# The last-ranked expert of a mixture moved to the third turn, with unsplit weights, in the two column halves of TensorE

## The reference, cut to what matters

```python
logits = (xt @ router).astype(jnp.float32)
top_logit, top_idx = lax.top_k(logits, TOP_K)          # 2 of 8 experts for each of 256 tokens
gates = jax.nn.softmax(top_logit, axis=-1)
...
out[token] += gate * ((silu(x @ w1[e]) * (x @ w3[e])) @ w2[e])   # w1, w3: 1024 x 1408, w2: 1408 x 1024
```

## Time and profile before

| what | before |
|---|---|
| median of 3 runs | 1899.74 us (1897.98 to 1900.82) |
| profiled execution | 1896.1 us, its span 1894.1 us |
| mean granted clock of TensorE | 0.988 |
| PE busy | 1841.9 us (97%) |
| DVE, ACT, POOL busy | 1331.0, 917.2, 63.0 us |
| HBM to SBUF, mean | 170 GB/s |

### The profile page before, as it was taken

The page is one execution under the profiler, slowest core; times in us unless marked ns, Lnnn a source line. Parts: engine busy times, 40 slices in busy tenths (PEclk is TensorE's granted clock), DMA queues, the critical chain, the costliest instruction groups (busy, mean ns, idle before and its releaser), DMA issues.

```text
span 1894.1 us, 35005 instructions
## 1 busy us (share of the span) xinstructions
PE 1841.9 (97%) x14961; PEld 1729.7 (91%) x14961; DVE 1331.0 (70%) x1900; ACT 917.2 (48%) x1072; POOL 63.0 (3%) x32
## 2 busy tenths in 40 slices
PE   9899999999998999999999999999999999989999
PEld 9889999999997999999999888888889988889988
DVE  7975566755589656667564768888879678666675
ACT  5353345433453433434434566777766544444453
POOL 0000000000000000000101010111110000000000
PEclk9899999999998999999999999999999999999999
DMA  8221246455542214535545578899965423324330
GB/s 316 91 90 57 90 167 222 162 193 180 181 159 90 74 57 139 193 138 189 194 154 187 200 238 291 323 332 329 337 249 180 154 90 102 124 99 159 122 122 24
DMA packets 52826, 321.89 MB, mean 170 GB/s; under 512 B 6336, under 2 KB 9664, under 8 KB 20032
## 3 DMA queue, kind: packets, MB, share of 16 engines
q1 hardware_dynamic: 52240, 317.76, 47.8%
q10 hardware_dynamic: 432, 1.90, 0.3%
HBM read 317.01 MB, written 1.05 MB: 168 GB/s over the span
## 4 chain that ended last, share of the span: by engine, by line
PE 80%; DVE 13%; ACT 4%; issue 3%; DMA 0%; POOL 0%; DVEq 0%; ACTq 0%; SPq 0%; POOLq 0%
PE b L393 78%; DVE s_arena L409 5%; DVE s_ring_lo L516 3%; ACT s_wh L418 2%; PE b L2553 1%; DVE s_arena L1442 1%; PE b L2089 0%; DVE s_arena L652 0%; DVE s_arena L412 0%; DVE s_arena L2588 0%; DVE s_roots L409 0%; ACT s_arena L418 0%; DMA s_ring<-experts 0%; POOL s_ring_lo L516 0%; DVE s_Hl L409 0%
## 5 line engine op out<-in xcount | busy, mean ns | idle before, releaser
L516 DVE TENSOR_TENSOR s_ring_lo<-s_ring,s_wh 128x2048 fp32r<-128x2048 f32 (+3 forms) x316 | 661.6, 2098 | 302.3 <-ACT s_wh L418 300.9
L418 ACT ACTIVATE s_wh<-s_ring 128x2048 fp32r<-128x2048 f32 (+3 forms) x332 | 574.1, 1732 | 273.7 <-PE b L393 265.9
L393 PE MATMUL b<-s_Hh,s_wh 128*128 128x256 f32 x2184 | 636.2, 291 | 3.8 <-DVE s_arena L409 1.2
L393 PE MATMUL b<-s_Hl,s_wh 128*128 128x256 f32 x2184 | 618.8, 283 | 0.0
L393 PE MATMUL b<-s_Hh,s_ring_lo 128*128 128x256 f32 x2184 | 618.6, 283 | 0.0
L393 PEld LDWEIGHTS b<-s_Hh,s_wh 128*128 128x128 f32 x2184 | 419.4, 192 | 13.6 <-issue 4.7
L393 PEld LDWEIGHTS b<-s_Hl,s_wh 128*128 128x128 f32 x2184 | 419.8, 192 | 1.1
L393 PEld LDWEIGHTS b<-s_Hh,s_ring_lo 128*128 128x128 f32 x2184 | 419.3, 192 | 0.0
L393 PE MATMUL b<-s_arena_r,s_wh 128*128 128x256 f32 x1536 | 277.0, 282 | 6.7 <-DVE s_arena L409 1.7
L393 PEld LDWEIGHTS b<-s_arena_r,s_wh 128*128 128x128 f32 x1536 | 235.5, 188 | 9.4 <-DVE s_arena L409 2.1
L393 PE MATMUL b<-s_arena_r,s_ring_lo 128*128 128x256 f32 x768 | 215.4, 280 | 0.0
(11 more groups left out here) (198 smaller groups left out, 1776.1 us busy)
## 6 DMA issues: line engine op xcount, KB each, us to landing
s_ring<-fixed SPq DMA_DIRECT2D x158, 1024.0 KB, 4.9
s_ring<-experts SPq DMA_DIRECT2D x95, 1024.0 KB, 5.3
s_ring<-experts SPq DMA_DIRECT2D x48, 768.0 KB, 4.6
s_ring<-fixed SPq DMA_DIRECT2D x24, 256.0 KB, 4.2
s_c<-c SPq DMA_DIRECT2D x1, 1664.0 KB, 17.6
s_ring<-fixed SPq DMA_DIRECT2D x3, 512.0 KB, 6.1
s_arena<-s_arena SPq DMA_DIRECT2D x48, 32.0 KB, 3.1
s_c<-c ACTq DMA_DIRECT2D x1, 1344.0 KB, 5.6
```

Source lines behind the costliest of these rows:

```text
L393: return e.matmul(out, l, r, start=start, stop=True, skip_group_check=True)
L418: return e.activation(out, x, ACT.Copy, scale=scale)
L516: e.tensor_tensor(l_, r_, h_.bitcast(F), SUB).then_inc(*up(engine, z % "lo", i))
```

## The change

Turn 2 is now the last-ranked expert, and ranks 2 to 6 follow as turns 3 to 7 (`RANK`). So the turn with two sets, whose second is packed, is turn 3. The new turn 2 (`NARROW`) has one set of at most 64 rows. Its tokens stay in full fp32 (`n_H`, `n_hid`), its 18 weight pieces are neither rounded nor split (`unsplit`), and each block of 128 rows of the contraction is one full-precision matmul with 64 stationary columns. Even blocks write partitions 0 to 63 of the bank, odd ones 64 to 127, and the two halves are added where the packed set adds its high and low sums (`packed_dve`, through `gate_low`, `up_low`) or, for w2, by the scatter, whose placing matrix holds the 64 places twice. The groups of the gathers become (2), (3), (4, 5), (6, 7).

```diff
-SETS = (2, 2, 2, 1, 1, 1, 1, 1)
+RANK = (0, 1, 7, 2, 3, 4, 5, 6)
+SETS = (2, 2, 1, 2, 1, 1, 1, 1)
 DENSE = 2
-GROUPS = ((2,), (3, 4), (5, 6), (7,))
+NARROW = 2
+GROUPS = ((2,), (3,), (4, 5), (6, 7))
...
             for j in range(0 if i == 0 else i + AHEAD, min(i + AHEAD + 1, len(LOADS))):
-                if j not in late_pieces:
+                if j not in late_pieces and j not in unsplit_pieces:
                     round_piece(e, j)
...
-        PACKED = {(2, 1)}
+        PACKED = {(3, 1)}
+        HALF = PACKED | {(NARROW, 0)}
...
         GATHERS = {1: [(0, 0), (0, 1), (0, 2), (0, 3)], 2: [(1, 0), (1, 1), (1, 2), (1, 3)],
-                   3: [(2, 0), (2, 1)], 4: [(2, 2), (2, 3)], 5: [(3, 0), (3, 1)], 6: [(3, 2), (3, 3)]}
+                   3: [(2, 0), (2, 1), (2, 2), (2, 3)], 4: [(3, 0), (3, 1)], 5: [(3, 2), (3, 3)]}
...
-                    out[9 + s if p > DENSE else 10 + s].append(("turn", p, 0, s))
-                    out[14 + s].append(("turn", p, 1, s))
+                    out[9 + s if p > DENSE else 11].append(("turn", p, 0, s))
+                    out[15 if p == NARROW else 14 + s].append(("turn", p, 1, s))
...
+        def unsplit(e, i):
+
+            e.wait_ge(landed[i % RAW], 16 * (i // RAW + 1))
+            return raw_of(i).rearrange("p (k n) -> p k n", k=LOADS[i].kt)
...
                 for kk in range(4):
+                    if p == NARROW:
+                        last = mm(e, b[HALVES[kk % 2], 0:width], n_H[:, 4 * h + kk, :], wv[:, kk, :], h == 0 and kk < 2)
+                        continue
...
                 for k in range(4 * j, min(4 * j + 4, 11)):
+                    if p == NARROW:
+                        last = mm(e, b[HALVES[k % 2], :], n_hid[:, k, :], wv[:, k - 4 * j, :], k < 2)
+                        continue
...
-                for half in range(2):
+                for half in range(2 if p != NARROW else 0):
                     rest_piece(e, li["xd", (p, half, 2)], "G")
```

More of the change, by code:

```diff
@@ L503, in build @@
         even_late = [li["eg", 0], li["eg", 1]] + [li["eo.2", j] for j in range(6)]
-        pool_pieces = {li["xd", (p, half, 2)] for p in range(8) for half in range(2)}
+        pool_pieces = {li["xd", (p, half, 2)] for p in range(8) for half in range(2) if p != NARROW}
+        unsplit_pieces = {j for j, piece in enumerate(LOADS) if piece.turn == NARROW}
         def rest_piece(e, i, engine):
@@ L526, in rests @@
             for j in range(0 if i == 0 else i + AHEAD, min(i + AHEAD + 1, len(LOADS))):
-                if j not in pool_pieces and j not in late_pieces:
+                if j not in pool_pieces and j not in late_pieces and j not in unsplit_pieces:
                     rest_piece(e, j, "V")
@@ L1824, in build @@
         GROUP_OF = {p: g for g, ps in enumerate(GROUPS) for p in ps}
-        PLACES = [sum(64 if (p, s) in PACKED else 128 for p in ps for s in range(SETS[p])) for ps in GROUPS]
+        half_units = [t for t, (p, ch, s) in enumerate(UNITS) if (p, s) in HALF]
+        PLACES = [sum(64 if (p, s) in HALF else 128 for p in ps for s in range(SETS[p])) for ps in GROUPS]
         GATHERS = {1: [(0, 0), (0, 1), (0, 2), (0, 3)], 2: [(1, 0), (1, 1), (1, 2), (1, 3)],
-                   3: [(2, 0), (2, 1)], 4: [(2, 2), (2, 3)], 5: [(3, 0), (3, 1)], 6: [(3, 2), (3, 3)]}
-        PLACED = {1: 0, 2: 1, 3: 2, 5: 3}
+                   3: [(2, 0), (2, 1), (2, 2), (2, 3)], 4: [(3, 0), (3, 1)], 5: [(3, 2), (3, 3)]}
+        PLACED = {1: 0, 2: 1, 3: 2, 4: 3}
         STEPS = 24
@@ L1871, in job_end @@
         def job_end(job):
+            if job[0] == "turn" and job[1] == NARROW or job[0] == "gather" and job[1] == GROUP_OF[NARROW]:
+                return {"turn": "hid hi", "gather": "slot hi"}[job[0]], *job[1:]
             return {"turn": "hid lo", "scatter": "spread", "gather": "slot lo", "place": "PT", "tokens": "token lo", "wide": "gates wide"}[job[0]], *job[1:]
@@ L2043, in place_pe @@
             for blk in range(2):
-                last = mm(e, b[:, 256:257], m_P[g % 2][:, blk, o:o + 128].bitcast(F), m_gp[:, blk, p:p + 1], blk == 0)
+                last = mm(e, b[:, 256:257], m_P[g % 2][:, blk, o:o + 128].bitcast(F), m_gp[:, blk, RANK[p]:RANK[p] + 1], blk == 0)
             last.then_inc(*up("PE", "P turned", p, s))
@@ L2150, in expert_down_pe @@
             i = li["xd", (p, half, j)]
-            wv = wts(i)
-            e.wait_ge(*on("lo", i))
+            if p == NARROW:
+                wv = unsplit(e, i)
+            else:
+                wv = wts(i)
+                e.wait_ge(*on("lo", i))
             for s in range(SETS[p]):
@@ L2424, in moe_dve @@
                     for job in jobs[i]:
+                        if job_end(job)[0] in ("hid hi", "slot hi"):
+                            continue
                         if job[0] == "tokens":
@@ L3347, in sync_program @@
                     e.wait_ge(*on("experts known"))
-                    who[piece.turn] = e.value_load(m_int[0:1, piece.turn:piece.turn + 1], min_val=0, max_val=7)
+                    who[piece.turn] = e.value_load(m_int[0:1, RANK[piece.turn]:RANK[piece.turn] + 1], min_val=0, max_val=7)
                 if i == 2:
```

42 lines of the change are left out of this document (25 added, 17 removed).

## The result

| what | before | after |
|---|---|---|
| median of the runs taken together | 1899.07 us (1894.9 to 1901.11, 6 runs) | 1885.34 us (1881.24 to 1890.11, 6 runs) |
| ratio | | 0.9932, 95% interval 0.9918 to 0.9945 |
| profiled execution | 1896.1 us, span 1894.1 | 1881.24 us, span 1879.3 |
| first to last 512-column matmul of the mixture | 1044.50 to 1393.17, 348.7 us | 1041.86 to 1378.41, 336.5 us |

What follows compares the result with a forecast made beforehand. PE was taken to bound the kernel: 16.4 us saved in products, less 2.4 for changes of shape and 1.5 for waits, gives -12.5 us. The forecast median was 1887.2 us, range 1882.5 to 1892.

Steps and rivals of the forecast that it cites:

- What bounds: Whole kernel: PE is the bound, busy 97% of the span; transfers are the next limit.
- The slot: Turn 2's products: an even and an odd block run side by side, 0.86 us at 512 columns, 29.3 us in all.
- Rival 3: Turn 2's products: the column halves take turns, products 56.8 us, time 1913, slower; chance 0.07.
- Changes of shape: PE switching to 64 columns and back: 0.14 us in, 0.09 out; with 64-partition runs and turned chunks, cost 2.4.
- Rival 2: Turn 2's slots: weight loads do not overlap and cost 9.7 us, leaving gain 2.8, time 1897; chance 0.03.
- The waits: PE in turns 2 and 3: narrow pieces cover less of other engines' work, together +1.5 us of waiting.
- the wait at `place`: Step 15 of turn 2: PE waits 1.1 us at the first `place` for ACT's and DVE's chain ending in the gather.
- the add: Second scatter of turn 2: PE waits 0.6 us for the add of the first scatter.
- the first split piece: Turn 3's first piece, rounded after the gather's copies: of the order of 0.3 us may show, inside the 1.1's error.
- Transfers: Turn 2 to turn 3's first piece: 7 MB land in 26 us against PE's 28, covered; bare, up to 4 us.
- Rival 4: Whole kernel: transfers fall behind and hand back the time saved, up to 1900, no gain; chance 0.04.
- Sum: Whole kernel: -16.4 + 2.4 + 1.5 = -12.5 us, profiled execution 1896.1 to 1883.6, median 1887.2.

Runs made afterwards that it cites:

- one half alone: The changed kernel with all of the unsplit expert's blocks in the left column half; 1909.19 us, ratio 1.0059.
- reordered version: The changed kernel with turn 3's first two scatters one step earlier and, ending turn 2, the next piece's rounding before the tanh; 1880.62 us, rerun 1886.62.
- both retimed: The changed kernel with turn 2's fourth gather and turn 3's first two scatters each one step earlier; 1888.41 us, ratio 0.9949.
- half the work: The changed kernel with two of four row blocks of every piece of the unsplit expert left out; 1887.19 us, ratio 0.9942.

## Why the prediction was right

Predicted were 1887.2 us (1882.5 to 1892), faster; measured 1885.34. By its steps:

- **What bounds.** Right for the kernel before, and for the changed one in the main: PE's busy time and the time fall together.
- **The slot.** 0.86 was right. Records of a slot start 0.43 us apart in pairs, and the 140 narrow records take 30.7 us from start to next start: the 29.3 of the sum, and what the changes of shape add inside the nine rows (0.05 at the first pair and 0.10 at the last of each). Rival 3 (in turns, 1913) is what one half alone costs, 1909.19, and it is not what two halves do. The forecast rested on two rows with 128 to 256 columns from a quiet arena; it held at 512 from a ring that was being written. The slot from which Rival 3 decides is 1.23 us by the prediction's own figures (41.8 over 28 and three quarters of 8), not 1.21; nothing hangs on it.
- **Changes of shape.** The way in costs the 0.14 that was taken: the first narrow matmul starts 0.20 or 0.21 us after the one before it, where 0.11 or 0.12 lie between starts of such matmuls, and the first pair takes 0.48 where the others take 0.43. The way out was mis-sized: the start after the last pair comes after 0.53, and the second of the wide gather matmuls behind it 0.19 or 0.22 after the first in place of 0.11 or 0.12, so 0.18 to 0.20 where 0.09 was taken. That is some 0.33 for both, up to 3.0 for nine against the 2.1 of the sum. What was removed made up for it: PE's time in fast 512- and 384-column matmuls is 46.7 us less, where 45.7 was said. The rule of the Trainium skill, "TensorEngine Tiling (Array Packing)", Key Properties, that a switch of mode drains the engine, agrees with these rows in that a start comes later both ways.
- **Weight loads.** Rival 2 did not happen. The Trainium skill's "TensorE: Matmul & The Clock Gate", Part 3, has a load overlap a matmul only if the row groups differ. Here both halves take all rows, and a slot of 0.86 us has no room for 0.27 of loads; the measurement decides.
- **The waits.** The sum was right, 1.6 us more than before (6.2 against 4.6 in the stretch) where 1.5 was said. Its parts: the gathers at steps 2 and 3 nothing (0.1 said), the wait at `place` 0.97 (1.1 said), the add 0.92 (0.6 said, mis-sized by 0.3), the first split piece 0.17 (0.3 said to lie inside the error). The old wait that was to go, 0.3, did not: the waits for X are still four, and sum to 1.9 with the 0.92 in it, 1.0 without, as before. Small waits elsewhere (for the turning, for POOL's low part) are 0.4 less, which had no entry in the sum. So in its parts the 1.5 owes something to luck.
- **The place of the wait.** The chain named for `place` (gate copy, sum, tanh, chunk, gather) is right, and the reordered version shows it: with the tanh behind, 0.97 is 0.41. What the prediction took for a side effect inside the error is the same chain's next link: the rounding of turn 3's first piece. Take the first wait away alone, as in *both retimed*, and 1.21 us stand before that piece.
- **Transfers.** "Covered either way" was right, but nearer than it reads. 28 us for PE against 26 bare; measured 27.75, share 0.97, and with PE's work cut by half 25.1. Turn 3's first piece lands 0.3 us before ACT comes to it. The time from issue to landing of a 1 MB piece rose (below) without a wait. Rival 4 is what the kernel has waiting behind a slot a little faster, not what it does.
- **Later turns.** As before: the last turn takes 67.4 us (1311.02 to 1378.41), before 67.5.
- **Sum.** -12.5 said; the stretch gives -12.1, PE's own time -13.8 (said -14.0), waits +1.6. With the new order of the turns one `place` product more lies in the stretch and one less ahead of it, 0.66 us that the sum rightly left alone: so the change itself gives -12.8, PE's own time -14.4. The other 2.0 us of the two profiled executions, 0.5 at the start and 1.5 at 207 us, are no step of the prediction.

## What to carry to other kernels

Unsplit full-precision matmuls pay here only with both column halves side by side, and what they save against packed, split weights is ScalarE's and VectorE's work, not TensorE's: look for the engine that has to prepare the operand. Put a stage that needs its operands fast ahead of one that needs them slowly: the same edit gave 13.7 us before the turn with two sets and 2.9 at the end. And when a wait is removed, follow the queue of the engine that ended it to the next thing behind: here the same 1 us came up again, and only another order on ScalarE and VectorE took 0.56 of it away.

## What the runs showed of the hardware

- **Landing times grow before anything waits.** The median from issue to landing, in turn 2 of before and of after:

```profile
s_ring<-experts SPq DMA_DIRECT2D x9, 1024.0 KB, 4.8
```

```profile
s_ring<-experts SPq DMA_DIRECT2D x9, 1024.0 KB, 8.3
```

In the run with half the work it is 12.5. Of PE's waits in turn 2 none in the changed kernel is for a transfer: the ring's depth absorbs the 3.5 us. The median shows a limit coming nearer while no wait does yet.

- **Both column halves stream different 512-column data, each at the rate that one has alone** (0.43 us for a pair of records, and 0.43 for one record with one half in use), and a matmul of the free half may start ahead of one that waits for the busy half, but not far ahead: even, even, odd, odd costs nothing (336.8 us), four and four costs 9.6 us. The Trainium skill, "TensorE: Matmul & The Clock Gate", Part 3, has matmuls start in strict order; by it three pieces of even, even, odd, odd would take, by an estimate, seven times 0.86 us, 6.0. They took 5.35, so the measurement differs from the rule here.
- **A wait can cost twice.** With packed weights the granted clock is 0.50 to 0.58 in four pieces of the stretch, which begin in or just behind waits of 2.0 to 3.7 us, and in the run with half the work there are two such spells of 10.2 us, the second in its wait of 7.5. In the changed kernel, whose waits are at most 1.6 us, it is 1.00 throughout the stretch. The length of one wait is not all: the first spell of the run with half the work begins in turn 2, behind waits of 1.0, 1.3 and 1.6 us.
- **The clock elsewhere makes the spread of this kernel.** Stretches of the same kernel agree within 0.2 us (336.55 and 336.72, 335.36 and 335.45), while the part behind them, the same in all, takes 500.9, 503.8, 500.9 and 505.3 us. In it the clock is at the lower level for 13.7, 20.5, 13.7 and 23.9 us, and half of what is added comes near the 2.9 and 4.4 us. So a change of 1 or 2 us in the mixture has to be read from the stretch.
